# A two-layer hybrid decoder step on one Trainium2 core: zero rows beside the up projection's tiles, gap tiles back to back, and two of them moved into the up projection

## The chip, the core and the metric

The kernel runs on one core of a Trainium2 chip. Its engines are TensorE (PE), VectorE (DVE), ScalarE (ACT), GpSimd (POOL) and SyncE (SP), which here only issues loads; all DMAs, whoever issues them, run on the core's 16 DMA engines. The metric is the device time of one launch in microseconds. PE's granted clock is given as a share of 2.4 GHz; it has two levels, 1.0 (2.4 GHz) and 0.5 (1.2 GHz).

## The reference

One inference step of a two-layer decoder for a prompt of 256 tokens and 8 sample tokens, 264 columns together, width 1024, all in float32. Layer 0 mixes with gated linear attention and ends with a dense SwiGLU (the up projection has 2 x 2816 columns); layer 1 mixes with stick-breaking attention over shared keys and values (the samples' keys lie in a paged cache) and ends with eight SwiGLU experts, two for each token. Each norm is modulated by shift, scale and gate vectors, which are a matrix product of the conditioning vectors c.

```python
def modulate(h, shift, scale):
    return h * (1 + scale[:, None, :]) + shift[:, None, :]
def shared_kv(x, c, kv_norm, kv_ada_w, kv_ada_b, kv_w):
    shift, scale = jnp.split(jax.nn.silu(c) @ kv_ada_w + kv_ada_b, 2, axis=-1)
    h = modulate(rmsnorm(x, kv_norm), shift, scale)
    k, v = jnp.split(h @ kv_w, 2, axis=-1)
    ...
def swiglu(h, w_gate_up, w_down):
    a, b = jnp.split(h @ w_gate_up, 2, axis=-1)
    return (jax.nn.silu(a) * b) @ w_down
# trunk, for each layer
    sh1, sc1, g1, sh2, sc2, g2 = jnp.split(jax.nn.silu(c) @ p['ada_w'][layer] + p['ada_b'][layer], 6, axis=-1)
    h = modulate(rmsnorm(x, p['norm_mix'][layer]), sh1, sc1)
    ...
    x = x + g1[:, None, :] * out
    h = modulate(rmsnorm(x, p['norm_ffn'][layer]), sh2, sc2)
    ...
```

## The kernel before

Activations lie transposed, 8 chunks of 128 rows by 264 columns. **Weights** come through a ring of three buffers of 2 MB. The list `STREAM` gives the order of all tiles: `gla_in`, `gla_out`, `ffn_up` (11), `ffn_down` (6), `sb_q` (2), `kv` (4), `sb_out`, the cached keys and values, and 32 `ada` tiles of the conditioning product. SP walks through it in order; before each load it waits until the tile that had the buffer is used up (`read_out`), and every later load stands behind that wait.

A weight tile is cut into four **units**. ACT casts a unit to `w_hi` (L1247), DVE takes the rest `w_lo` (L1604), and PE multiplies it in three products (`three`, L733 to L735), 24 matmuls per unit. `AHEAD` is 3: units are split three ahead of their use. When the fourth unit of a tile has its `w_lo`, its ring buffer is free. Four PSUM banks (0 to 3) take turns as the products' targets.

An **ada tile** is read by PE as it is, in eight matmuls of 32 rows (L704, four for each half); ACT copies the sums to `ada_row` (L1263), which has two halves, PE turns them (four transpositions, L688), and DVE adds them up into `mod` (`ada_add`, L1620 and L1621) and counts up `ada_kept`. `ADA_GROUPS` gives the tiles their PSUM banks.

Ahead of the up projection, of `sb_q` and of `kv` (stages `FFN0`, `MIX1`, `KV`) there is a **gap**: squares and sums (L723) of the new x, then DVE (L1662, L1671) and ACT (L1302) make the normed input chunk by chunk. In the kernel before each gap holds two ada tiles (`BEHIND_SUMS`: 16, 18 and 20 are the first ones): PE reads the first and half of the second, waits for ACT's copy, turns it, reads the other half, and only then starts the projection; the second one is turned behind the projection's first block. `KV` has no sums of its own, and its gap stands behind the turning of the query (L935).

**POOL** sets eight parts of `routed` to zero (L568 to L571), 0.5 MB each, as soon as the up projection's input is done, one behind the other; then it makes constants for the attention. Later it stores the samples' query (L586), spreads its rows over the partitions (L595), and multiplies the second page of each sample's cached keys (L606), while DVE multiplies the first (L1883), sums both up (L1885, L1890) and splits the units of `kv` in between.

`ada_kept` must reach `ADA_NEEDED` for a stage: 20 for `KV`, 26 for `FFN1`.

## Time and profile before

| | |
|---|---|
| median of 3 runs | 1775.8 us (1775.76 to 1776.41) |
| the profiled execution's own time | 1775.7 us |
| its span, first to last instruction | 1774.0 us |
| PE busy | 1618.1 us, 91% |
| DVE, ACT, POOL busy | 71%, 61%, 5% |
| mean granted clock | 0.954 |
| DMA | 546.24 MB, 308 GB/s |

The stages in the trace: conditioning and linear attention to about 240 us, its output projection to 262, first gap, up projection from 276, down projection to 483, second gap, `sb_q` to 523, third gap and `kv` to 600, attention to 680, then router and experts to the end. A busy share is a mean over such stages; what a wait costs is read where it stands.

### The profile page before, as it was taken

The page shows a single profiled execution, that of the slowest core. Times are in us where ns is not written, and L with a number is a line of the kernel's source. Part 1 is how long each engine was busy: PE and PEld are TensorE (multiplying, and loading weights), DVE is VectorE, ACT ScalarE, POOL GpSimd, SP SyncE. Part 2 cuts the span into 40 slices and gives each one's busy share as a digit, 9 for nine tenths or more (in the row PEclk, how much of TensorE's full clock was granted, in tenths as well). Part 3 has the DMA queues.
Part 4 walks back from the last instruction along what each step waited for, and adds up shares of the span by engine and source line. Part 5 has one row for each costly group of instructions (what it writes and reads, how often), then busy time and mean ns, then how long its engine had stood idle before and what let it go on. Part 6 is the DMA issues. An engine that isn't in the chain of part 4 may idle for free.

```text
span 1774.0 us, 25158 instructions
## 1 busy us (share of the span) xinstructions
PE 1618.1 (91%) x9156; PEld 1308.3 (74%) x9156; DVE 1263.9 (71%) x1433; ACT 1079.6 (61%) x1309; POOL 88.9 (5%) x135
## 2 busy tenths in 40 slices
PE   5799786999986799599999999999999999999992
PEld 2695265999976667278888888888888888888882
DVE  2463354554565724389899899899998998998982
ACT  2553133443452453477777777777777777777771
POOL 2000101000002400100000000000000000000001
PEclk9899887999998899899999999999999999999995
DMA  9266977555557887699999999999999999999972
GB/s 347 76 211 231 387 262 257 188 174 177 178 190 289 321 323 255 251 352 361 369 378 375 376 369 377 380 371 366 382 372 372 373 376 380 367 366 387 373 279 97
DMA packets 241091, 546.24 MB, mean 308 GB/s; under 512 B 6131, under 2 KB 28785, under 8 KB 241026
## 3 DMA queue, kind: packets, MB, share of 16 engines
q1 hardware_dynamic: 229202, 504.42, 78.4%
q0 software_dynamic: 11184, 38.75, 5.9%
q10 hardware_dynamic: 640, 2.18, 0.4%
q8 instruction: 45, 0.74, 0.2%
q14 instruction: 20, 0.16, 0.0%
HBM read 522.56 MB, written 22.75 MB: 307 GB/s over the span
## 4 chain that ended last, share of the span: by engine, by line
PE 83%; DMA 7%; DVE 5%; ACT 3%; issue 2%; POOL 1%; SPq 0%; another core or an unknown queue 0%; ACTq 0%; DVEq 0%; POOLq 0%
PE psum L733 24%; PE psum L734 24%; PE psum L735 24%; DMA ring<-in_ada_w 3%; PE psum L704 2%; DMA ring<-in_cache_k 2%; PE psum L1168 1%; DMA ring<-in_ffn_w_gate_up 1%; PE psum L723 1%; DVE w_lo L1604 1%; DVE ring L1883 1%; DMA ring<-in_gla_w_in 1%; PE psum L688 1%; PE psum L972 1%; ACT w_hi L1247 0%
## 5 line engine op out<-in xcount | busy, mean ns | idle before, releaser
L2055 DVE TENSOR_TENSOR w_lo<-ring,w_hi 128x1024 fp32r<-128x1024 f32 x672 | 814.2, 1224 | 81.7 <-ACT w_hi L1546 64.7
L1546 ACT CAST w_hi<-ring 128x1024 fp32r<-128x1024 f32 x672 | 706.6, 1054 | 206.2 <-PE psum L735 200.1
L733 PE MATMUL psum<-w_hi,xe_hi 128*128 128x512 f32 x896 | 359.9, 402 | 3.2 <-DVE w_lo L2055 3.2
L735 PE MATMUL psum<-w_hi,xe_lo 128*128 128x512 f32 x896 | 355.8, 397 | 0.0
L734 PE MATMUL psum<-w_lo,xe_hi 128*128 128x512 f32 x896 | 355.7, 397 | 0.0
L733 PE MATMUL psum<-hh,w_hi 128*128 128x264 f32 x864 | 252.8, 293 | 32.4 <-DVE w_lo L1604 19.7
L1604 DVE TENSOR_TENSOR w_lo<-ring,w_hi 128x1024 fp32r<-128x1024 f32 (+1 forms) x132 | 160.2, 1222 | 151.6 <-ACT w_hi L1247 151.4
L734 PE MATMUL psum<-hl,w_hi 128*128 128x264 f32 x864 | 249.2, 288 | 0.0
L735 PE MATMUL psum<-hh,w_lo 128*128 128x264 f32 x864 | 249.1, 288 | 0.0
L1247 ACT CAST w_hi<-ring 128x1024 fp32r<-128x1024 f32 (+1 forms) x132 | 135.6, 1034 | 127.7 <-PE psum L735 86.0
L733 PEld LDWEIGHTS psum<-w_hi,xe_hi 128*128 128x128 f32 x896 | 169.3, 189 | 42.5 <-DVE w_lo L2055 3.5
L735 PEld LDWEIGHTS psum<-w_hi,xe_lo 128*128 128x128 f32 x896 | 169.1, 189 | 41.1
L734 PEld LDWEIGHTS psum<-w_lo,xe_hi 128*128 128x128 f32 x896 | 169.4, 189 | 38.8
L733 PEld LDWEIGHTS psum<-hh,w_hi 128*128 128x128 f32 x864 | 167.5, 194 | 39.6 <-DVE w_lo L1604 28.0
L733 PE MATMUL psum<-w_hi,at_hi 128*128 128x512 f32 x448 | 179.0, 399 | 0.0
L734 PE MATMUL psum<-w_lo,at_hi 128*128 128x512 f32 x448 | 177.5, 396 | 0.0
L735 PE MATMUL psum<-w_hi,at_lo 128*128 128x512 f32 x448 | 177.5, 396 | 0.0
L734 PEld LDWEIGHTS psum<-hl,w_hi 128*128 128x128 f32 x864 | 167.8, 194 | 0.0
L735 PEld LDWEIGHTS psum<-hh,w_lo 128*128 128x128 f32 x864 | 166.6, 193 | 0.0
L735 PEld LDWEIGHTS psum<-w_hi,at_lo 128*128 128x128 f32 x448 | 84.4, 188 | 20.6
L734 PEld LDWEIGHTS psum<-w_lo,at_hi 128*128 128x128 f32 x448 | 84.5, 189 | 19.8
L733 PEld LDWEIGHTS psum<-w_hi,at_hi 128*128 128x128 f32 x448 | 84.4, 188 | 19.8
(347 smaller groups left out, 1421.3 us busy)
## 6 DMA issues: line engine op xcount, KB each, us to landing
ring<-in_moe_w_gate_up SPq DMA_DIRECT2D x112, 2048.0 KB, 9.2
ring<-in_moe_w_down SPq DMA_DIRECT2D x56, 2048.0 KB, 8.4
ring<-in_ada_w SPq DMA_DIRECT2D x24, 2048.0 KB, 10.9
ring<-in_ffn_w_gate_up SPq DMA_DIRECT2D x22, 1024.0 KB, 8.9
ring<-in_gla_w_in SPq DMA_DIRECT2D x6, 2048.0 KB, 11.2
ring<-in_kv_ada_w SPq DMA_DIRECT2D x4, 2048.0 KB, 8.0
ring<-in_ffn_w_down SPq DMA_DIRECT2D x4, 2048.0 KB, 7.9
ring<-in_kv_w SPq DMA_DIRECT2D x4, 2048.0 KB, 12.8
```

What stands on the lines that cost most here:

```text
L688: last = eng.transpose(pb[ADA_BANKS[i]][:, j * P:(j + 1) * P], ada_row[:, i % 2, j * P:(j + 1) * P], ident[:])
L704: last = eng.matmul(pb[ADA_BANKS[i]][g * STRIP:(g + 1) * STRIP, :], c_pad[:, k, :], cols8(slot("ada", i))[:, k, :], start=j == 1, stop=j == 3)
L723: last = eng.matmul(pb[7][:, 0:T], ones[:], h[:, k, :], start=k == 0, stop=k == KC - 1)
L733: eng.matmul(to, wh, ah, start=start, stop=False)
L734: eng.matmul(to, wh, al, start=False, stop=False)
L735: return eng.matmul(to, wl, ah, start=False, stop=stop)
L972: eng.matmul(pb[2 * (g % 2) + a][:, 0:384], neg_after[:], lg[:, a, :], start=False, stop=False, skip_group_check=True)
L1168: last = eng.transpose(pb[4 if p % 2 == 0 else 7][:, j * CAP:(j + 1) * CAP], act_e[:, j * P:(j + 1) * P], ident[:])
L1247: eng.copy(unit(w_hi, kind, m, ks), quarter(slot(kind, i), kind, m % 4, ks)).then_inc(S["hi_ready"], 1)
L1546: eng.copy(unit(w_hi, kind, n), quarter(ring[(BASE + j // 4) % RING], kind, j % 4)).then_inc(S["hi_ready"], 1)
L1604: eng.tensor_tensor(unit(w_lo, kind, m, ks), quarter(slot(kind, i), kind, m % 4, ks), unit(w_hi, kind, m, ks), ALU.subtract).then_inc(S["l ...
L2055: eng.tensor_tensor(unit(w_lo, kind, n), quarter(ring[(BASE + j // 4) % RING], kind, j % 4), unit(w_hi, kind, n), ALU.subtract).then_inc(S ...
```

## The change

- `STREAM`: ada tiles 18 and 19 are loaded ahead of up tiles 4 and 7 (`BESIDE_UP`); 20 and 21 take their place between the two `sb_q` tiles; between the `kv` tiles there is none. So the ring buffers are dealt out anew.
- PE: in the gaps of `FFN0` and `MIX1` both ada tiles are read whole, one right behind the other, and turned behind the first and the second block of the projection (`turn_behind`). Tiles 18 and 19 are read at the head of up tiles 4 and 7 and turned behind the first block of these. The gap of `KV` has no ada tile.
- ACT and DVE: copies and sums follow, the first copy of a gap one chunk later.
- POOL: zero write e waits until the units ahead of up tile e + 2 are used.

```diff
--- before.py
+++ after.py
@@ -62,18 +62,19 @@
 ADA_ORDER = [*range(16), *range(24, 28), *range(16, 24), *range(28, 32)]
 
 
-ADA_GROUPS = ((0, (0, 1)), (4, (2, 3)), (16, (4, 5)), (18, (4, 5)), (20, (6, 7)), (22, (6, 7)), (28, (2, 3)))
-BEHIND_SUMS = {FFN0: 16, MIX1: 18, KV: 20}
+ADA_GROUPS = ((0, (0, 1)), (4, (2, 3)), (16, (4, 5)), (18, (4, 5)), (20, (4, 5)), (22, (6, 7)), (28, (2, 3)))
+BEHIND_SUMS = {FFN0: (16, 17), MIX1: (20, 21), KV: ()}
+BESIDE_UP = {4: 18, 7: 19}
 ADA_STARTS = [start for start, _ in ADA_GROUPS]
 ADA_BANKS = [[banks for start, banks in ADA_GROUPS if start <= i][-1][i % 2] for i in range(len(ADA_ORDER))]
 ADA_NEEDED = {MIX0: 4, FFN0: 12, MIX1: 16, KV: 20, FFN1: 26, FINAL: 32}
 
 STREAM = ([("ada", i) for i in range(4)] + [("gla_in", i) for i in range(6)] + [("ada", i) for i in range(4, 16)]
           + [("gla_out", i) for i in range(2)] + [("ffn_up", 0), ("ada", 16), ("ada", 17)]
-          + [("ffn_up", i) for i in range(1, 11)]
+          + [t for i in range(1, 11) for t in ([("ada", BESIDE_UP[i])] if i in BESIDE_UP else []) + [("ffn_up", i)]]
           + [("ffn_down", i) for i in range(6)]
-          + [("sb_q", 0), ("ada", 18), ("ada", 19), ("sb_q", 1)]
-          + [("kv", 0), ("ada", 20), ("ada", 21), ("kv", 1), ("k_cache", 0), ("kv", 2), ("k_cache", 1), ("kv", 3), ("k_cache", 2), ("k_cache", 3)]
+          + [("sb_q", 0), ("ada", 20), ("ada", 21), ("sb_q", 1)]
+          + [("kv", 0), ("kv", 1), ("k_cache", 0), ("kv", 2), ("k_cache", 1), ("kv", 3), ("k_cache", 2), ("k_cache", 3)]
           + [("ada", 22)] + [t for i in range(4) for t in (("ada", 23 + i), ("v_cache", i))] + [("ada", 27)]
           + [("sb_out", i) for i in range(2)] + [("ada", i) for i in range(28, 32)])
 TILE_AT = {k: n for n, k in enumerate(STREAM)}
@@ -568,6 +569,7 @@
             eng.memset(zero_rows[:], 0.0).then_inc(S["consts"], 1)
             eng.wait_ge(S["consts"], 12 + STRIPS)
             for e in range(NE):
+                eng.wait_ge(S["unit_used"], UNIT_AT["ffn_up", e + 2])
                 eng.dma_start(routed[e * T:e * T + CAP, :], zero_rows[0:CAP, :]).then_inc(S["routed_zero"], 16)
             eng.wait_ge(S["routed_zero"], 16 * NE)
             eng.tensor_copy(ident_r[:], ident[:]).then_inc(S["att_consts"], 1)
@@ -688,6 +690,30 @@
                     last = eng.transpose(pb[ADA_BANKS[i]][:, j * P:(j + 1) * P], ada_row[:, i % 2, j * P:(j + 1) * P], ident[:])
                 last.then_inc(S["ada_turned"], 1)
 
+            def ada_strips(i, half):
+
+                for g in range(STRIPS):
+                    k = half * STRIPS + g
+                    last = eng.matmul(pb[ADA_BANKS[i]][g * STRIP:(g + 1) * STRIP, :], c_pad[:, k, :],
+                                      cols8(slot("ada", i))[:, k, :], start=half == 0, stop=half == 1)
+                    if half == 1:
+                        last.then_inc(S["ada_done"], 1)
+
+            def ada_whole(i):
+                landed(eng, "ada", i)
+                ada_strips(i, 0)
+                ada_strips(i, 1)
+
+            def ada_behind(m):
+
+                eng.wait_ge(S["ada_kept"], BEHIND_SUMS[m][0])
+                for i in BEHIND_SUMS[m]:
+                    ada_whole(i)
+
+            def turn_behind(m, i):
+                if i < len(BEHIND_SUMS[m]):
+                    ada_turn(BEHIND_SUMS[m][i])
+
             def ada(lo, hi, ends=False):
 
                 for u in range(lo, hi):
@@ -699,12 +725,7 @@
                     if j == 1:
                         landed(eng, "ada", i)
                     if j % 2 == 1:
-                        for g in range(STRIPS):
-                            k = (j // 2) * STRIPS + g
-                            last = eng.matmul(pb[ADA_BANKS[i]][g * STRIP:(g + 1) * STRIP, :], c_pad[:, k, :],
-                                              cols8(slot("ada", i))[:, k, :], start=j == 1, stop=j == 3)
-                            if j == 3:
-                                last.then_inc(S["ada_done"], 1)
+                        ada_strips(i, j // 2)
                     if j == 1 and i not in ADA_STARTS:
                         ada_turn(i - 1)
                 if ends:
@@ -892,9 +913,18 @@
 
 
             sum_squares(FFN0)
-            ada(64, 72)
+            ada_behind(FFN0)
+
+            def behind_up(i):
+                turn_behind(FFN0, i)
+                if i % 4 == 0 and i // 4 in BESIDE_UP:
+                    ada_turn(BESIDE_UP[i // 4])
+
             for i in range(11):
-                project("ffn_up", i + 1, IN_FFN, first=i, then=lambda i: ada_turn(17) if i == 0 else None)
+                if i in BESIDE_UP:
+                    eng.wait_ge(S["ada_kept"], BESIDE_UP[i])
+                    ada_whole(BESIDE_UP[i])
+                project("ffn_up", i + 1, IN_FFN, first=i, then=behind_up)
             for i in range(2 * DOWN_ROWS):
                 half, r = i // DOWN_ROWS, i % DOWN_ROWS
                 ks = chunks_of("ffn_down", i)
@@ -914,8 +944,8 @@
 
 
             sum_squares(MIX1)
-            ada(72, 80)
-            project("sb_q", 2, IN_Q, then=lambda i: ada_turn(19) if i == 0 else None)
+            ada_behind(MIX1)
+            project("sb_q", 2, IN_Q, then=lambda i: turn_behind(MIX1, i))
 
             def turn_kv(i):
 
@@ -929,16 +959,12 @@
                 last.then_inc(S["kv_turned"], 1)
 
             eng.wait_ge(S["kept_act"], empt[BLOCK_AT["sb_q", 7]][1])
-            eng.wait_ge(S["ada_kept"], 20)
+            eng.wait_ge(S["ada_kept"], 22)
 
             for j in range(8):
                 last = eng.transpose(pb[4 + j // 4][0:NB, (j % 4) * P:(j % 4 + 1) * P], kvq[:, 16 + j, TP:T], ident[:])
             last.then_inc(S["qs_turned"], 1)
-            ada(80, 88)
-
             def behind_kv(i):
-                if i == 0:
-                    ada_turn(21)
                 if i in TURN_AFTER:
                     if TURN_AFTER[i] == 0:
                         eng.wait_ge(S["ada_kept"], 22)
@@ -1301,9 +1327,10 @@
                         eng.wait_ge(S["scaled"], m * KC + k + 1)
                         eng.activation(hh[:, k, 0:TP], h[:, k, 0:TP], ACT.Identity,
                                        bias=mod[:, SHIFT[m] + k, 0:1]).then_inc(S["hh_ready"], 1)
-                        if k == 3:
-                            ada_copy(BEHIND_SUMS[m])
-                    ada_copy(BEHIND_SUMS[m] + 1)
+                        if k == 4 and BEHIND_SUMS[m]:
+                            ada_copy(BEHIND_SUMS[m][0])
+                    for i in BEHIND_SUMS[m][1:]:
+                        ada_copy(i)
                     return
                 for k in range(KC + 1):
                     if k < KC:
@@ -1420,6 +1447,8 @@
             eng.wait_ge(S["state_stored"], 16)
             for i in range(FFC + 1):
                 if i < FFC:
+                    if i % 2 == 0 and i // 2 in BESIDE_UP:
+                        ada_copy(BESIDE_UP[i // 2])
                     got = block("ffn_up", 2 * i)
                     if i >= 2:
                         eng.wait_ge(S["kept_dve"], empt[BLOCK_AT["ffn_up", 2 * i - 4]][1])
@@ -1835,7 +1864,6 @@
                 add_block("gla_out", i, GATE[MIX0])
 
             norm(FFN0)
-            ada_add(16)
 
             for i in range(S0):
                 eng.wait_ge(S[f"s0_stored{i}"], 16 * len(range(i, NB, S0)))
@@ -1844,7 +1872,10 @@
                 if i < FFC:
                     n, u = BLOCK_AT["ffn_up", 2 * i + 1], UNIT_AT["ffn_up", i // 2] + i % 2 * 2
                     if i == 1:
+                        ada_add(16)
                         ada_add(17)
+                    if i % 2 == 1 and i // 2 in BESIDE_UP:
+                        ada_add(BESIDE_UP[i // 2])
                     split(u + AHEAD)
                     split(u + 1 + AHEAD)
                     eng.wait_ge(S["unit_used"], u + 2)
@@ -1861,17 +1892,16 @@
                 for j in range(4):
                     add_block("ffn_down", 4 * half + j, GATE[FFN0])
             norm(MIX1)
-            ada_add(18)
             link(eng.memset(zs, 0.0))
             eng.wait_ge(S["att_consts"], 4 + 2 * STRIPS)
             eng.tensor_copy(bias_r[:], sb_bias[:]).then_inc(S["bias_ready"], 1)
             eng.wait_ge(S["bias_ready"], 1)
             eng.tensor_tensor(bias_r[SD:P, :], sb_bias[SD:P, :], bias_r[SD:P, :], ALU.subtract).then_inc(S["bias_ready"], 1)
             split_during("sb_q", 1)
-            ada_add(19)
+            ada_add(20)
+            ada_add(21)
             split_during("sb_q", 2, first=1)
             norm(KV)
-            ada_add(20)
 
             by_head = lambda v: v.rearrange("p (h d) -> p h d", h=SH)
             page_of = lambda b, page: slot("k_cache", b // 2)[:, (b % 2 * 2 + page) * D:(b % 2 * 2 + page + 1) * D]
@@ -1890,8 +1920,6 @@
                 eng.tensor_reduce(zs[:, 1, b, 0:SH], by_head(page_of(b, 1)), AX.X, ALU.add).then_inc(S["z_s_ready"], 1)
 
             for u in range(16):
-                if u == 1:
-                    ada_add(21)
                 if u in PAGES_DURING:
                     page, b = PAGES_DURING[u]
                     (page1_scores if page else page0_scores)(b)
```

SP's order of loads from up tile 1 on (`in_kv_ada_w` is ada 18 and 19, `in_ada_w` x2 is 20 and 21), before:

```order
L460 DMA ring<-in_ffn_w_gate_up 128x8x256 x20
L464 DMA ring<-in_ffn_w_down 128x8x512 x2
...
L469 DMA ring<-in_sb_w_q 128x8x512
...
L455 DMA ring<-in_kv_ada_w 128x8x512
...
L469 DMA ring<-in_sb_w_q 128x8x512
L469 DMA ring<-in_kv_w 128x8x512
L455 DMA ring<-in_ada_w 128x8x512 x2
L469 DMA ring<-in_kv_w 128x8x512
L448 ISA
L448 DMA ring<-in_cache_k 128x1024
```

and of the changed kernel:

```order
L461 DMA ring<-in_ffn_w_gate_up 128x8x256 x6
...
L456 DMA ring<-in_kv_ada_w 128x8x512
L461 DMA ring<-in_ffn_w_gate_up 128x8x256 x6
...
L456 DMA ring<-in_kv_ada_w 128x8x512
L461 DMA ring<-in_ffn_w_gate_up 128x8x256 x8
...
L470 DMA ring<-in_sb_w_q 128x8x512
L456 DMA ring<-in_ada_w 128x8x512 x2
L470 DMA ring<-in_sb_w_q 128x8x512
L470 DMA ring<-in_kv_w 128x8x512 x2
L449 ISA
L449 DMA ring<-in_cache_k 128x1024
```

Two ada loads stand between up loads, and the first cached keys no longer stand behind a load that waits for the key projection.

PE between the first gap's sums and the first unit of the up projection, before:

```order
L723 MATMUL psum<-h,ones 128x264 x8
L704 MATMUL psum<-ring,c_pad 32x512 x12
L688 MATMUL psum<-ident,ada_row 128x128 x4
L704 MATMUL psum<-ring,c_pad 32x512 x4
L733 MATMUL psum<-hh,w_hi 128x264
```

and of the changed kernel:

```order
L744 MATMUL psum<-h,ones 128x264 x8
L697 MATMUL psum<-ring,c_pad 32x512 x16
L754 MATMUL psum<-hh,w_hi 128x264
L755 MATMUL psum<-hl,w_hi 128x264
L756 MATMUL psum<-hh,w_lo 128x264
```

The transposition is gone from between the ada matmuls, and the projection follows at once.

DVE from the last chunk of the key input to the first page product, before:

```order
L1671 SCALAR_TENSOR_TENSOR hl<-h,mod,hh 128x256 x2
L1620 TENSOR_REDUCE mod<-psum 128x36
L1621 TENSOR_TENSOR mod<-mod,vec_a 128x36
L1604 TENSOR_TENSOR w_lo<-ring,w_hi 128x1024
L1620 TENSOR_REDUCE mod<-psum 128x36
L1621 TENSOR_TENSOR mod<-mod,vec_a 128x36
L1883 TENSOR_TENSOR ring<-ring,h 128x1024
```

and of the changed kernel:

```order
L1700 SCALAR_TENSOR_TENSOR hl<-h,mod,hh 128x256 x2
L1633 TENSOR_TENSOR w_lo<-ring,w_hi 128x1024
L1913 TENSOR_TENSOR ring<-ring,h 128x1024
L1915 TENSOR_REDUCE work<-ring 128x16
L1633 TENSOR_TENSOR w_lo<-ring,w_hi 128x1024
```

Both sums are gone from there.

## Rows read from the trace of the kernel before

**Rows 1.** Windows: us, busy of each engine (instructions), PEclk, DMA share, GB/s.
```profile
289.40:299.60 10.20, 0.00 (x0) 0.03 (x1) 1.71 (x3) 2.78 (x4) 2.58 (x12) 0.61 1.07 355
299.60:483.20 183.60, 182.95 (x1488) 182.74 (x1488) 100.41 (x134) 79.94 (x110) 0.00 (x0) 0.98 0.59 194
...
522.70:555.70 33.00, 17.71 (x145) 14.04 (x144) 13.93 (x29) 12.44 (x23) 6.20 (x6) 0.83 0.68 252
```

**Rows 2.** Chain of waits, first gap and up projection: start us, us, what.
```profile
277.00 1.06 ACT w_hi L1247
...
278.17 1.24 DVE w_lo L1604
...
279.43 0.37 SPq L460
...
279.84 16.96 DMA ring<-in_ffn_w_gate_up
...
296.82 1.05 ACT w_hi L1247
...
299.61 0.56 PE psum L733
```

**Rows 3.** DMA queues, 278 to 298 us: packets, MB, share of 16 engines.
```profile
q0 software_dynamic: 1152, 4.19, 56.9%
q1 hardware_dynamic: 2799, 2.83, 41.7%
```

**Rows 4.** Up loads: 330 to 352 us (KB each, median us to landing), and line L460.
```profile
ring<-in_ffn_w_gate_up SPq DMA_DIRECT2D x4, 1024.0 KB, 6.8
...
DMA to landing us min/median/max: 5.2/8.9/19.2
```

**Rows 5.** Chain of waits, third gap and kv: start us, us, what.
```profile
533.59 0.37 SPq L469
...
535.88 15.26 DMA ring<-in_cache_k
551.16 1.24 DVE ring L1883
...
612.86 0.88 DVE work L1909
```

**Rows 6.** Second gap and sb_q: timelines of SP and DVE, line L469 at 500, chain.
```profile
500.38 0.37 SPq L469 DMA_DIRECT2D ring<-in_sb_w_q  x1
...
501.42 3.58 SPq L455 DMA_DIRECT2D ring<-in_ada_w  x1
...
DMA to landing us min/median/max: 8.1/8.1/8.1
...
497.11 0.48 DVE L1671 SCALAR_TENSOR_TENSOR hl<-h,mod,hh 128x256 fp32r<-128x256 f32 x1 [0.18 <-ACT hh L1302]
...
510.83 0.39 PE psum L733
```

**Rows 7.** Timeline of PE: a half ada tile, a turn, and the end of sb_q.
```profile
626.64 1.06 PE L704 MATMUL psum<-ring,c_pad 128*32 128x512 f32 x8
...
627.64 0.43 PE L956 MATMUL psum<-bias_r,sixty_fourth 128*128 128x384 f32 x1
...
501.48 0.60 PE L688 MATMUL psum<-ident,ada_row 128*128 128x128 f32 x4
501.83 0.37 PE L733 MATMUL psum<-hh,w_hi 128*128 128x264 f32 x1
...
522.61 0.14 PE psum L735
```

**Rows 8.** Windows of 2 us around the hole at 290, columns as in rows 1.
```profile
290.00:292.00 2.00, 0.00 (x0) 0.00 (x0) 0.00 (x0) 0.00 (x0) 0.00 (x0) 0.91 1.07 370
...
304.00:306.00 2.00, 2.00 (x13) 2.00 (x13) 0.00 (x0) 0.74 (x2) 0.00 (x0) 0.68 1.10 348
```

**Rows 9.** GpSimd's query rows: timeline, landing (530 to 550 us), landing in the whole kernel.
```profile
534.10 1.12 POOL L595 DMA_DIRECT2D h<-q_scratch  x2 [1.86 <-DMA q_scratch<-work]
...
DMA to landing us min/median/max: 7.7/9.2/10.7
...
DMA to landing us min/median/max: 3.6/5.5/10.7
```

## The prediction

> **What bounds the kernel now.** I read the page's 40 slices first: PE is busy nearly everywhere, with dips around 280 to 300 us and 520 to 600 us. The expert loop behind 760 us runs whole and isn't touched, so only the stretch from 262 to 614 us counts, and everything later moves with it.
>
> The windows by stage give the sizes [rows 1]. From 289.40 to 299.60 PE does no matmul at all, while the DMA engines run at a share of 1.07. From 299.60 to 483.20 PE is busy for 182.95 of 183.60 us: up and down projection are bound by PE. From 522.70 to 555.70 PE works 17.71 of 33.00 us.
>
> The chain of waits names the cause of the first hole [rows 2]. ACT and DVE split the last quarter of up tile 0, which frees its ring slot. SP issues up tile 1 at 279.43, its load takes 16.96 us from 279.84, and PE resumes only at 299.61. In the same stretch GpSimd's queue writes the zero rows, 4.19 MB in eight DMAs, against 2.83 MB of loads [rows 3]. Later, with nothing beside them, up loads land in a median of 6.8 us [rows 4].
>
> The chain also names the second hole [rows 5]. SP issues key tile 1 at 533.59, and behind it the first cached key pages, whose load is the 15.26 us to 551.16, where DVE begins the page products. From there to the first softplus at 612.86 the chain is almost all DVE products, reductions and splits, with a page load between.
>
> **The change, part by part.** Times of before are of the profiled execution, 1775.7 us (span 1774.0), against a median of 1775.8; the two agree, so differences go straight onto the median.
>
> (1) Zero rows. Each of the eight writes now waits until an up tile is used (tiles 1 to 8), so none lies beside up tile 1. Behind these waits GpSimd has only the remaining writes and the constants of the attention; they are wanted at about 498 us, and the last wait ends near 400. The load of up tile 1 is issued at about 279.0: ACT's copy of the second ada tile no longer waits for PE, which brings its next split forward by 0.4 us, and DVE's behind it [rows 2]. The load then takes between 6.8 us (the later median) and 13.6 us (twice that, since two more tiles are queued behind it on the same queue). sb_q tile 1 shows the nearest case, three 2 MB tiles the first issued at 500.38 and the last at 501.42, the first landing 8.1 us after its issue [rows 6]. I take 8. It lands at 287.0, and from the landing to PE's first matmul there were 2.79 us (296.82 to 299.61) [rows 2]. PE resumes at 289.8 instead of 299.61: 9.8 us. I keep 9.5, because both ada additions now stand on DVE in front of the next split (0.5 us, half of it behind PE).
>
> (2) Both gap tiles back to back in the first gap. PE's first up unit was held until 276.3 by the transposition and the last four ada matmuls; now it starts with the first ready chunk, near 271.5, and ends with the last chunk, near 277. With 3.0 us per unit (seven units in the 20.9 us from 501.83 to 522.70 [rows 7]) and two transpositions of 0.35 us, PE has used units 0 to 3 by 286.8. The tile lands later than that, so this part is worth nothing in time. It is hidden under the load.
>
> (3) Ada tiles 18 and 19 inside the up projection. PE is the bound there, so this is a full price. Four ada matmuls (eight records, two for each in fp32) hold PE for 1.0 us (626.64 to 627.64) and a transposition for 0.35 (501.48 to 501.83) [rows 7]: per tile 2 x 1.0 + 0.35, for two tiles 4.7 us. The new waits: PE's for the sums of the tile before is met a tile earlier; ACT's copy waits for the last ada matmul, and behind it stands a split that PE wants three units on, 2.0 + 0.6 + 1.05 + 1.23 = 4.9 us against 2.0 + 9.0. ACT's copy and DVE's sum fit into their idle time, each of them being busy for about half of this stretch (79.94 and 100.41 of 183.60 us [rows 1]). Where they were, behind the sums of the key input, PE had nothing else to do, so taking them out there returns nothing on PE.
>
> The loads: with an ada tile in a ring of three, an up tile is often issued when the tile two before it has been split, not three. From the split of a tile's last unit to that of the first unit two tiles later lie five units, 14.5 us, plus 6.4 us of units split ahead (three units less a split's 2.3 us). Loads of this kind took 5.2 to 19.2 us, the longest beside the zero rows [rows 4]; a 0.5 MB write beside each adds some 1.5 us. Nothing waits: cost 0, the cover being the 20.9 us.
>
> (4) Gap of sb_q. Tiles 20 and 21 are now read back to back, their turns lie behind units 0 and 1, and PE's wait ahead of the query's turning is for sums that DVE has by 514 us, nine before it gets there. PE's first unit is paced by DVE's last chunk at 497.11 to 497.59 [rows 6] and ends near 498.0; units 1 to 3 and both turns end at 507.7. But unit 4 needs sb_q tile 1, issued at 500.38 after a split; the split comes 0.45 us sooner, so unit 4 starts at 510.3 instead of 510.8. Earlier PE just met it; now it idles 2.6 to 3 us. Idle time has a price in the clock. After 289.4 the granted clock fell to the lower level (1.2 GHz) within 290 to 292, and after the restart at 299.61 it came back only within 304 to 306 [rows 8]. Such a low stretch, some 5.7 us, costs 2.8 us at half speed. Here it would come on the path. Between -0.45 (no fall) and +2.4 (a full one) I take +1.0. The Trainium skill, "TensorE: Matmul & The Clock Gate", Part 1, speaks against this edit in the same way: the gate goes to half rate after idling, and where it falls is run-variable because the monitor runs free. By that page either end can come, -0.45 or +2.4; the trace agrees that idling brings the lower level, and no run yet shows how the fall varies.
>
> (5) Key gap. The key tiles 0 and 1 and the first key pages no longer stand behind ada tiles 20 and 21. Key pages 0 take the slot of sb_q tile 1, free at about 515, behind 6 MB that runs out near 518, so they land near 524 instead of 551.16. What is late next is the queries' rows: the products need them spread over all partitions, and GpSimd stores the query only after ACT's two copies. One ada copy ahead of these is gone (0.46 us), so the row loads start at 533.65 instead of 534.10. Before, the three loads of that place landed 7.7, 9.2 and 10.7 us after issue, the first being the one that is needed; over the whole kernel such loads range from 3.6 to 10.7 with a median of 5.5 [rows 9]. I take 7.5, a little under the row of this place: DVE starts at 541.1 instead of 551.16, 10.0 us earlier. With 5.5 it is 12, with 10.7 it is 6.8. Everything up to 612.86 is the same sequence on DVE, with the same loads issued from the same releases, and moves whole.
>
> A rule of the skill sharpens this price: "DMA: Bandwidth & Descriptors", Queues, rings and completion order, says an engine round-robins between queues packet by packet. A row load then shares with one load on SP's queue as badly as with three queued there, so the landing stays 7.7 us and the gain 9.8, not 12. The trace agrees so far as two queues were served side by side in the first hole, 4.19 MB and 2.83 MB over the same 20 us [rows 3].
>
> Sum: -9.5 + 4.7 + 1.0 - 10.0 = -13.8 us. 1775.8 - 13.8 = 1762.
>
> **The rivals.**
> A: the query rows become late. At a landing of 10.7 us the fifth part gives 6.8, and 1765; if they needed 17.5 us nothing would be left of it, and 1772. For it: three loads on a second queue landed 7.7 to 10.7 us after issue. Against: there were 6 MB beside them, now 2. Chance 0.08 for a time of 1766 to 1772.
>
> B: the zero writes do their harm again, 0.5 MB at a time. Eight writes at about 350 GB/s are 1.5 us each, 12 us if all lay on the path: 1774, no change. For: the same engines. Against: the loads of the up projection are idle for part of each tile (194 GB/s used [rows 1], up to 350 to be had), so only with the prefetch gone would it show. Chance 0.04.
>
> C: slower than before, one mechanism: the ring. Ada tiles 18 and 19 take a buffer each, six up tiles have only 20.9 us of cover. It decides from a landing above that: at 23.2 us the six waits eat the 13.8 us, at 25 they cost 6 x 4.1 = 24.6 us and give 1786. For: 19.2 us occurred. Against: that was beside all zero rows at once; the median is 8.9 [rows 4]. Chance 0.05.
>
> D: the clock does better. If the hole behind unit 3 of the up projection is short enough for no fall (3 us by my count, 286.8 to 289.8), another 2.8 us go, and without a fall in sb_q 1.4 more: 1758. If in addition the query rows land in 5.5 us, 1756. Chance 0.2.
>
> **How the numbers follow.** Forecast as it stands (1759 to 1766) 0.63, A 0.08, B 0.04, C 0.05, D 0.2. The predicted time is 1762. The range 1755 to 1769 holds the forecast, D and half of A, some 0.87 by these counts, less what I haven't thought of. A change under 0.2% (3.6 us) couldn't be told from none. Faster by more: forecast, D, and most of A, 0.91. Within: 0.04. Slower: 0.05.
>
> **What would show it.** The load of up tile 1 at about 8 us with no write beside it, and PE's hole behind unit 3 at 3 us instead of 10.2; if the load still takes over 13 us, the zero rows were not the cause. Sixteen ada matmuls and eight transposition matmuls between up tiles, the up and down projection longer by 4.7 us, without a new idle of PE for a split; a wait of ACT for up loads there means C. A short idle of PE between the fourth and fifth unit of sb_q, with the granted clock behind it. DVE's first page product released by the query rows and not by the key pages, at about 10 us less behind the last chunk of the key input, and the same 61.7 us from there to the first softplus. Wrong would be a key page load that still releases it, or a gain of under 6 us there.

## The result, and the profile after

The changed kernel takes 1760.03 us (median of 4 runs, 1758.68 to 1763.92) against 1776.1 us for the kernel before in the same series (4 runs, 1775.76 to 1776.41): a ratio of 0.9914, interval 0.9902 to 0.9926. The forecast was 1762. The profiled execution took 1761.09 us, its span being 1759.3 us, 14.7 us less than the span before.

The chain of waits in the first gap of the changed kernel (start us, us, what) answers to [rows 2]:

```profile
276.45 0.95 ACT w_hi L1273
...
277.53 1.24 DVE w_lo L1633
278.78 0.37 SPq L461
...
279.19 7.78 DMA ring<-in_ffn_w_gate_up
287.00 1.05 ACT w_hi L1273
...
289.79 0.36 PE psum L754
```

The load of up tile 1 takes 7.78 us, not 16.96. The DMA queues from 278 to 298 us (packets, MB, share of 16 engines) say why: GpSimd's queue q0, 4.19 MB there in [rows 3], is gone, and SP's queue moves 6.20 MB in place of 2.83.

```profile
q1 hardware_dynamic: 6137, 6.20, 96.7%
q8 instruction: 1, 0.02, 0.4%
```

The windows over PE's hole, over up and down projection, and over the key gap, with the columns of [rows 1]:

```profile
286.80:289.80 3.00, 0.02 (x2) 0.04 (x1) 1.73 (x3) 2.80 (x4) 0.00 (x0) 1.00 1.10 348
289.80:475.90 186.10, 185.45 (x1528) 182.07 (x1528) 101.47 (x141) 80.91 (x112) 7.54 (x20) 1.00 0.70 237
516.20:540.20 24.00, 14.78 (x105) 12.69 (x105) 13.13 (x25) 11.73 (x21) 6.21 (x6) 0.94 0.44 156
```

The hole is 3.0 us and the granted clock in it stays at 1.00; before it was 10.2 us at 0.61. The 186.1 us behind it hold 40 more matmul records (1528 against 1488): four fp32 ada halves and two turns. PE stays busy for 185.45 of them.

One of the two ada tiles, in PE's timeline (start us, us, engine, line, operation); its neighbours are up matmuls on both sides, with no idle time in front:

```profile
324.54 0.28 PE L756 MATMUL psum<-hh,w_lo 128*128 128x264 f32 x1
324.76 1.92 PE L697 MATMUL psum<-ring,c_pad 128*32 128x512 f32 x16
...
326.61 0.39 PE L754 MATMUL psum<-hh,w_hi 128*128 128x264 f32 x1
326.84 0.28 PE L755 MATMUL psum<-hl,w_hi 128*128 128x264 f32 x1
...
329.52 0.28 PE L756 MATMUL psum<-hh,w_lo 128*128 128x264 f32 x1
329.64 0.60 PE L690 MATMUL psum<-ident,ada_row 128*128 128x128 f32 x4
330.00 0.37 PE L754 MATMUL psum<-hh,w_hi 128*128 128x264 f32 x1
330.21 0.28 PE L755 MATMUL psum<-hl,w_hi 128*128 128x264 f32 x1
```

In sb_q PE now idles before unit 4, where before it just met it (510.83 in [rows 6]). PE's timeline, and windows of 2 us behind it:

```profile
502.70 0.39 PE L754 MATMUL psum<-hh,w_hi 128*128 128x264 f32 x1 [2.08 <-DVE w_lo L1633]
```

```profile
502.00:504.00 2.00, 1.30 (x7) 1.30 (x8) 2.00 (x3) 2.00 (x4) 0.00 (x0) 0.77 1.06 388
504.00:506.00 2.00, 2.00 (x11) 2.00 (x10) 1.93 (x6) 1.07 (x2) 0.00 (x0) 0.50 1.05 385
506.00:508.00 2.00, 2.00 (x17) 2.00 (x16) 1.13 (x1) 0.56 (x2) 0.00 (x0) 0.88 1.05 386
```

The idle time is followed by a stretch at the lower clock level, 1.2 GHz. Against the full clock these windows lose 2 x (0.23 + 0.50 + 0.12) = 1.7 us.

In the key gap the chain no longer goes through the key pages ([rows 5]) but through the query's store and row loads (start us, us, what):

```profile
524.55 2.67 DMA q_scratch<-work
...
527.51 8.03 DMA h<-q_scratch
...
535.62 1.24 DVE ring L1913
...
551.16 6.78 DMA ring<-in_cache_k
...
573.60 6.60 DMA ring<-in_cache_k
...
597.89 0.88 DVE work L1937
```

The stretch as a whole, cut at marks that are the same instructions in every kernel: "sums 1" is PE's first squares matmul behind gla_out, "resume" its first matmul of up tile 1, "sums 2" the first one behind the down projection, "key input" DVE's first operation on it (h<-x,rstd), "page" the first page product, "softplus" the first softplus. Times are differences between row starts of the timelines, in us of one profiled execution each; of after they are 262.12, 289.79, 475.92, 516.21, 535.62 and 597.81.

| kernel | sums 1 to resume | to sums 2 | to key input | to page | to softplus | sum |
|---|---|---|---|---|---|---|
| before | 37.44 | 183.62 | 39.60 | 28.33 | 61.62 | 350.61 |
| after | 27.67 | 186.13 | 40.29 | 19.41 | 62.19 | 335.69 |
| difference | -9.77 | +2.51 | +0.69 | -8.92 | +0.57 | -14.92 |

The whole difference of the spans is in this stretch. It is also a better ruler than the total, which went from 1773.16 to 1778.61 us over the 30 runs of the kernel before in the experiments' series. But each sum is one execution, and a fall of the clock inside it moves it by some 1.5 to 2.6 us (e10).

### The profile page after: what moved, and what is told of

It is laid out like the page before. It is cut to its first block, busy times and chain, and to the rows that moved or that the text cites. A ratio compares the mean times of both kernels' runs of the same rounds, so it can differ in the third digit from the quotient of the medians.

```text
span 1759.3 us, 25141 instructions
## 1 busy us (share of the span) xinstructions
PE 1618.5 (92%) x9156; PEld 1307.5 (74%) x9156; DVE 1262.0 (72%) x1433; ACT 1078.2 (61%) x1309; POOL 89.4 (5%) x135
## 4 chain that ended last, share of the span: by engine, by line
PE 76%; issue 9%; DMA 7%; DVE 4%; ACT 2%; POOL 1%; SPq 0%; POOLq 0%; ACTq 0%; DVEq 0%
PE psum L754 22%; PE psum L755 22%; PE psum L756 22%; DMA ring<-in_ada_w 3%; PE psum L697 2%; PE psum L1194 1%; DMA ring<-in_gla_w_in 1%; DVE ring L1913 1%; DVE w_lo L1633 1%; DMA ring<-in_cache_k 1%; PE psum L744 1%; PE psum L998 1%; PE psum L690 1%; DMA routed<-h_tok,row_of 1%; PE psum L1188 1%
```

## The experiments

Totals are medians; each ratio is to the kernel before in the same series, whose median was 1774.89 us for e1 to e4, 1775.31 for e5 to e8 and 1776.06 for e9 to e11; "sum" is the stretch from sums 1 to softplus as above.

| run | total (lowest to highest) | ratio to before, interval | sum |
|---|---|---|---|
| e1 zero wait alone | 1762.97 (1761.97 to 1765.33) | 0.9934 [0.992, 0.9947] | 339.55 |
| e2 zero rows at once | 1770.77 (1769.27 to 1772.35) | 0.9975 [0.9964, 0.9985] | 346.58 |
| e3 turn in the gap | 1759.81 (1758.64 to 1760.28) | 0.9911 [0.9896, 0.9926] | 334.30 |
| e4 tiles back | 1763.66 (1762.67 to 1768.41) | 0.9942 [0.9928, 0.9955] | 338.67 |
| e5 zero rows twice | 1758.98 (1757.35 to 1763.34) | 0.9916 [0.9902, 0.9929] | 335.62 |
| e6 kept busy | 1763.07 (1761.74 to 1763.61) | 0.9928 [0.9914, 0.9941] | 335.23 |
| e7 query early | 1752.82 (1750.12 to 1754.07) | 0.9872 [0.9857, 0.9887] | 329.23 |
| e8 split early | 1752.82 (1751.34 to 1753.82) | 0.9872 [0.9857, 0.9887] | 329.01 |
| e9 both | 1746.58 (1745.79 to 1748.17) | 0.9836 [0.9823, 0.985] | 319.31 |
| e10 rows behind the tile | 1760.12 (1759.74 to 1762.1) | 0.991 [0.9897, 0.9924] | 335.02 |
| e11 both, turn in the gap | 1750.5 (1746.45 to 1752.84) | 0.9848 [0.9833, 0.9862] | 326.20 |

**e1: the zero wait alone**, on the kernel before.

```diff
             for e in range(NE):
+                eng.wait_ge(S["unit_used"], UNIT_AT["ffn_up", e + 2])
                 eng.dma_start(routed[e * T:e * T + CAP, :], zero_rows[0:CAP, :]).then_inc(S["routed_zero"], 16)
```

> The kernel before with one edit: each zero write waits until up tile e + 2 is used. Theory (the zero rows held up tile 1): the load falls from 16.96 us to about 8, the tile is there at 287.9, and PE, which ends unit 3 at 289.4, resumes near 290.6 instead of 299.61: 9 us; with a hole of 1.2 us instead of 10.2 the clock has no reason to fall, another 2.8 us. Together 9 to 12 us: 1764 to 1767. Rival (the load is slow because two more 2 MB tiles are queued behind it, 13 us or more): the tile lands at 293 or later, and the gain is under 4 us: 1772 or more.

The load took 7.88 us. PE's timeline has a hole of 1.18 us, and the windows over the hole and over up and down projection read, with the columns of [rows 1]:

```profile
290.15 0.36 PE L734 MATMUL psum<-hh,w_hi 128*128 128x264 f32 x1 [1.18 <-DVE act L1855]
```

```profile
288.90:290.10 1.20, 0.08 (x1) 0.00 (x0) 1.20 (x3) 1.20 (x3) 0.00 (x0) 1.00 1.10 347
290.10:471.20 181.10, 180.39 (x1488) 180.20 (x1488) 100.44 (x135) 80.00 (x110) 8.79 (x20) 1.00 0.65 220
```

The same 1488 matmuls that took 182.95 us at a clock of 0.98 take 180.39 at 1.00. So one line is worth 11.1 us of the sum: 9.1 of load (37.44 to 28.35) and 2.5 of clock (183.62 to 181.07), less 0.6 elsewhere. The total, 1762.97 us, lies 1 us under the expected 1764 because the kernel before took 1774.89 us in this series; the gain, 11.9 us, is within the expected 9 to 12. The rival fell.

**e2: the zero rows at once**, the added wait of e1 taken out of the changed kernel.

```diff
-                eng.wait_ge(S["unit_used"], UNIT_AT["ffn_up", e + 2])
```

> The changed kernel without the waits of the zero writes, so all eight are issued right behind the last chunk of the up projection's input. Theory: the load of up tile 1 takes 16 to 17 us again instead of 7.8, PE resumes at 296 + 2.8 = 299 instead of 289.8, 9 us, and the clock falls in a hole of 12 us, 2.8 us more: 1769 to 1772. Rival (the new order of the gap shortened the load, not the writes): the load stays near 8 us and the time near 1760.

4.19 MB of zeros lie beside 2.30 MB of loads again, and PE idles for 12.67 us. PE's timeline, and windows of 2 us in the hole:

```profile
301.15 0.56 PE L753 MATMUL psum<-hh,w_hi 128*128 128x264 f32 x1 [12.67 <-DVE act L1884]
```

```profile
290.00:292.00 2.00, 0.00 (x0) 0.00 (x0) 0.00 (x0) 0.00 (x0) 0.00 (x0) 0.66 1.04 413
292.00:294.00 2.00, 0.00 (x0) 0.00 (x0) 0.00 (x0) 0.00 (x0) 0.00 (x0) 0.50 1.03 332
```

The sum is 10.9 us longer than after's, 9.67 to the resume and 1.4 behind it. The new order of the gap did nothing for the duration of the load.

**e3: the turn in the gap**, the changed kernel with the old order inside the first two gaps.

```diff
-            ada_behind(FFN0)
+            ada(64, 72)
...
-            ada_behind(MIX1)
+            ada(80, 88)
```

(and the turns, copies and sums of these tiles where they were)

> The changed kernel with the old order inside the first two gaps: the first ada tile is turned between the halves of the second, and only the second one's turn lies behind unit 0. Theory: worth nothing in the first gap, since up tile 1 lands at 287 either way (PE ends unit 3 near 289 instead of 286.8, and the hole of 3 us closes); in the gap of sb_q PE ends unit 3 some 2 us later, just in time for tile 1, and with no hole the clock stays up. So 1760 less 0 to 1.5 us, and a smaller spread than the 5 us of the changed kernel. Rival (back to back tiles start the units earlier and this is kept): 2 to 3 us slower, 1762 to 1763.

PE's hole in the up projection shrinks to 0.74 us and the one in sb_q is gone; there the clock stays at 1.00 from 496 to 508. The total is the same as after's within its spread, 1759.81 against 1760.03, and the rival (2 to 3 us slower) fell. The sum is 1.4 us shorter. PE resumes 0.65 us later behind sums 1, because up tile 1 is issued 17.26 us behind them and not 16.66; the key input is reached 0.7 us sooner behind sums 2, and the page product 1.0 sooner behind that, half of it the row's landing (7.51 us). So back to back tiles brought 0.6 us in the first gap and cost 0.7 in the second: as long as the next tile was late, they mostly turned paced work into idle time.

**e4: the tiles back**, ada tiles 18 and 19 in the gap of sb_q, 20 and 21 in the key gap.

```diff
-BEHIND_SUMS = {FFN0: (16, 17), MIX1: (20, 21), KV: ()}
-BESIDE_UP = {4: 18, 7: 19}
+BEHIND_SUMS = {FFN0: (16, 17), MIX1: (18, 19), KV: (20, 21)}
+BESIDE_UP = {}
```

> The changed kernel with ada tiles 18 and 19 in the gap of sb_q and 20 and 21 in the key gap again (back to back, turned behind the next units); nothing lies in the up projection. Theory: up and down projection 5.3 us shorter, and the first page product again released by the key pages' load, 8.9 us later: 1760 + 3.6 = 1763.6. Rival A (what the two tiles cost on PE in the up projection is more than their matmuls, through the ring): the up projection gets shorter by more than 5.3 us, and the whole is no slower than 1760. Rival B (the gain of the key gap came from elsewhere): the page product is not late, and the time is near 1755.

1763.66, as the theory had it. From the resume to sums 2 it takes 181.05 us (e1: 181.07), so the two tiles cost 186.13 - 181.06 = 5.1 us in the up projection, and nothing through the ring. The key pages' load is back in the chain, and the page product is 28.3 us behind the key input, not 19.4:

```profile
523.98 15.11 DMA ring<-in_cache_k
```

In sb_q PE idles here for 2.28 us, a little longer than in after, and yet the granted clock stays at 1.00 behind it (PE's timeline and a window):

```profile
498.82 0.39 PE L754 MATMUL psum<-hh,w_hi 128*128 128x264 f32 x1 [2.28 <-DVE w_lo L1635]
```

```profile
500.00:502.00 2.00, 2.00 (x19) 2.00 (x18) 1.93 (x5) 1.20 (x2) 0.00 (x0) 1.00 1.05 386
```

From sums 2 to the key input it takes 38.96 us, 1.3 us less than after.

**e5: the zero rows twice**, a second 0.5 MB behind each write.

```diff
+                eng.dma_start(expert_out[e * CAP:(e + 1) * CAP, :], zero_rows[0:CAP, :]).then_inc(S["routed_zero"], 16)
```

> The changed kernel with each zero write doubled (a second 0.5 MB behind it, of the same zeros, into rows that are rewritten later). Theory (the loads of the up projection have cover enough): nothing waits, 1760 within 1 us. Rival B (a write beside an up load delays PE): what eight more writes of 1.5 us cost, up to 12 us, 1772.

The sum is 335.62 against 335.69. Rival B of the prediction fell.

**e6: kept busy**, extra matmuls in PE's two holes.

```diff
+            def keep_busy(n):
+                for _ in range(n):
+                    eng.matmul(pb[6][:, 0:P], ones[:], ident[:], start=True, stop=True)
```

> The changed kernel with extra matmuls, whose sums nobody reads, in PE's two holes: 12 of 128 columns in fp32 behind unit 3 of the up projection (some 2.5 us of the 3) and 8 behind unit 3 of sb_q (1.7 us of 2.1). Theory (an idle of 2 us brings the lower clock in some executions): the granted clock stays at 1.00 from 500 to 508 us, where it cost 0.23 + 0.50 + 0.12 of 2 us each = 1.7 us, so 1758.3, and the runs lie within 2 us of each other instead of 5. Rival (the clock falls for what lies earlier, in the paced first unit of sb_q, not for the hole): 1760 and the same spread.

Half right, and the half that is right isn't shown to come from the matmuls. The windows in sb_q show the full clock with 16 records of extra matmuls ahead of them, where after had 0.77 and 0.50:

```profile
502.00:504.00 2.00, 0.46 (x5) 0.27 (x3) 1.25 (x2) 2.00 (x4) 0.00 (x0) 1.00 1.06 389
504.00:506.00 2.00, 1.97 (x16) 1.97 (x17) 2.00 (x2) 2.00 (x4) 0.00 (x0) 1.00 1.04 384
```

But in e4 and e10 the clock stayed up behind unfilled holes of 2.28 and 1.91 us, so one execution doesn't show that the extra matmuls held it; they end ahead of the landing, and 1.57 us of the hole are left. And in this execution sb_q tile 1 landed later (ACT had waited 10.12 us for it, 8.84 in after), and only 0.5 us of the sum is left of the gain. The total is not better but 3 us worse, and the stretch to softplus doesn't hold those 3 us; they lie later, around the router (the chain reaches the first expert matmul at 742.97, after's at 739.37), where its chain of waits has a piece "another core or an unknown queue" of 4.55 us. Why isn't settled. The five runs lie within 1.9 us of each other, as the theory had it; but e10, with its holes, stays within 2.4 us and e11, without them, spreads over 6.4, so the scatter isn't shown to come from the holes. From softplus to the end of the span alone the profiled runs differ by 4.5 us (1159.35 in e1, 1163.89 here).

**e7: the query early**, ACT's two copies of the query inside the loop over the key input's chunks.

```diff
+                        if m == KV and k == 1:
+                            eng.wait_ge(S["qs_turned"], 1)
+                            eng.copy(qs_tok[:, 0:512], pb[4][0:NB, :])
+                        if m == KV and k == 3:
+                            eng.copy(qs_tok[:, 512:D], pb[5][0:NB, :]).then_inc(S["qs_kept"], 1)
```

> The changed kernel with ACT's two query copies inside the loop over the key input's chunks (behind chunks 1 and 3) instead of behind chunk 7, so that the query is stored while the chunks are still made. Theory (the query rows release the first page product): the store is done before the last chunk, the row loads are issued at 523.9 instead of 527.5 and the page product starts at 532 instead of 535.6, 3.6 us; ACT's copies hold some chunks back by up to 0.6 us. 1756.5 to 1757. Rival A (a key page or a split is late next): under 1 us gained. Rival B (the delayed chunks reach PE and the splits behind): no gain or slower.

Twice the expected gain: the page product is 12.38 us behind the key input, not 19.41. 3.1 us are the earlier issue (8.18 us behind the key input, 11.30 in after), 3.9 a landing of 4.1 instead of 8.0, which the expectation did not have. What the row loads wait for is now DVE's last chunk and no longer the store. In after SP's key tile 2 was issued at 526.49, a microsecond ahead of the rows at 527.51. Here the order is the other way round (timelines of GpSimd, SP and DVE, one kernel):

```profile
523.68 1.12 POOL L597 DMA_DIRECT2D h<-q_scratch  x2 [2.89 <-DVE hl L1702]
...
524.82 0.39 SPq L470 DMA_DIRECT2D ring<-in_kv_w  x1
...
527.88 1.23 DVE L1915 TENSOR_TENSOR ring<-ring,h 128x1024 f32<-128x1024 f32 x1 [3.08 <-DMA h<-q_scratch]
```

**e10: the rows behind the tile**, e7 with the row loads held until the split that releases key tile 2.

```diff
+            eng.wait_ge(S["lo_ready"], UNIT_AT["kv", 0] + 4)
             for b in range(Q_ROWS - 1):
                 load_q(b)
```

> The kernel with the early query copies, but GpSimd's row loads wait for the split that releases key tile 2, so they are issued beside or just behind that 2 MB load (524.8) instead of 1.1 us ahead of it (523.7). Theory (what the loads wait for is the 2 MB tile issued first: the row took 8.0 us behind it in the changed kernel and 4.1 us ahead of it in this one): the landing goes back to about 8 us, the page product starts at 532.5 instead of 527.9, 4 to 5 us for a delay of 1.1: 1757. Rival (the landing was short for another reason, such as the store being long done): 4 us again, 1 us slower than with the early copies alone, 1754.

```profile
527.75 0.39 SPq L470 DMA_DIRECT2D ring<-in_kv_w  x1
...
528.31 1.12 POOL L597 DMA_DIRECT2D h<-q_scratch  x2 [4.59 <-DVE w_lo L1636]
...
536.05 1.23 DVE L1916 TENSOR_TENSOR ring<-ring,h 128x1024 f32<-128x1024 f32 x1 [8.33 <-DMA h<-q_scratch]
```

The store had been issued 5.2 us earlier (it took 2.67 us in after), and still the row took 7.65 us (chain of waits), 0.56 us behind the tile. From the key input to the page product it is 17.62 us against 12.38: 1.7 us of later issue and 3.5 of landing. The rival fell: what is issued first decides. The other profiled executions agree. With the rows 1.1 us ahead of the tile they landed in 4.10, 4.14 and 4.17 us (e7, e9, e11), with the rows 0.5 to 1.0 us behind it in 7.51 to 8.19 us (after, e3, e5, e6, e8, e10).

The total, 1760.12 us, is 3 us above the expected 1757. One piece of it lies elsewhere: from the resume to sums 2 this execution takes 188.79 us, where every other one with the same matmuls and a short hole or none takes 186.05 to 186.15. PE's hole in the first gap is as long as after's, but here the clock fell behind it, and in sb_q, where it fell in after, it did not (38.84 us from sums 2 to the key input). PE's timeline, and windows behind the hole:

```profile
290.80 0.56 PE L755 MATMUL psum<-hh,w_hi 128*128 128x264 f32 x1 [2.88 <-DVE act L1888]
```

```profile
290.00:292.00 2.00, 1.21 (x5) 1.24 (x6) 1.93 (x7) 2.00 (x4) 0.00 (x0) 0.50 1.10 347
294.00:296.00 2.00, 2.00 (x11) 2.00 (x11) 1.63 (x3) 0.00 (x0) 0.00 (x0) 0.50 1.09 346
```

Against e7 the two together make 1.1 us of the sum; the rest of the 3 us isn't located. After's sum and this one's are alike (335.69 and 335.02) only because such pieces cancel.

**e8: the split early**, unit 3 of up tile 0 and of sb_q tile 0 split between ACT's squares.

```diff
+                    if k == 6:
+                        for n in EARLY.get(m, ()):
+                            split(n, late=True)
                     eng.activation(h[:, k, :], x[:, k, :], ACT.Square).then_inc(S["squared"], 1)
```

(and on DVE ahead of its wait for the sums)

> The changed kernel with the split of unit 3 of up tile 0 and of sb_q tile 0 made in the gap before, between ACT's squares 5 and 6 and, on DVE, ahead of the mean, both idle there. Up tile 1 is then issued near 266 instead of 278.8, sb_q tile 1 near 480 instead of 492.6. Theory: both holes of PE go, 3.0 and 2.1 us, and with the second one the low clock behind it (1.7 us): 1760 - 5 to -6.8, 1753 to 1755. Rival (two more 2 MB tiles beside the first make it land no earlier than PE needs it, or the split delays the sums): a gain under 2 us.

SP issues up tile 1 3.8 us behind sums 1 (261.52), in after it was 16.7, and PE is busy for 199.83 of the 201.40 us from its first up matmul to sums 2. SP's timeline (one row for six DMAs) and the window:

```profile
265.32 12.80 SPq L463 DMA_DIRECT2D ring<-in_ffn_w_gate_up  x6
```

```profile
270.70:472.10 201.40, 199.83 (x1632) 194.99 (x1632) 108.61 (x155) 89.45 (x125) 8.49 (x21) 1.00 0.68 229
```

The sum is 6.7 us shorter: 3.2 up to sums 2, 2.6 in the gap of sb_q, 1.0 behind the page product. The rival fell; neither the sums nor the first landing suffered.

**e9: both**, the edits of e7 and e8 together.

> The changed kernel with both edits together: the splits of unit 3 made in the gaps before, and the query copies inside the chunk loop. Theory (separate places on the path): from the sums of the first gap to the first softplus 335.7 us less 6.5 (query) and less 6.7 (splits), 322.5 us, and 1746 to 1747 in all. Rival (with the early splits sb_q ends sooner and the key pages come to be late instead of the query rows): 2 us or more of it are lost, 1749.

1746.58 us, the best version, 13.5 us below the changed kernel. The sum is 319.31, 3.2 us below what the two gains add up to, since the key input is reached 1.2 us sooner behind sums 2 than in e8 (there the clock is at 0.50 to 0.67 from 482 to 490 us; here it is back at 1.00 from 488 on) and the two page loads behind the first product land faster (6.13 and 6.10 us against 6.78 and 6.60 in after; chain of waits):

```profile
518.08 4.14 DMA h<-q_scratch
522.30 1.24 DVE ring L1922
...
537.93 6.13 DMA ring<-in_cache_k
...
559.70 6.10 DMA ring<-in_cache_k
...
582.16 0.88 DVE work L1946
```

**e11: both, with the turn in the gap**, the edit of e3 on top of e9.

> Both edits as before, and the first two gaps in the old order: the first ada tile turned between the halves of the second. Theory (back to back tiles were worth nothing only because up tile 1 was late): now no tile is late, PE starts the units at 276.5 instead of 271 and ends unit 3 at 290.0 instead of 286.8, 3 us in each of the two gaps: 5 to 6 us slower than with both edits alone, near 1752. Rival (the order of the gap never matters): the same time as with both edits.

Slower than e9 by 3.9 us in the median and 6.9 in the sum, of which 2.5 lie up to sums 2 and 1.9 in the gap of sb_q; the rest, 2.4, is behind the page product. The profiled execution is the slowest of the five, and two of the five (1746.45 and 1746.83) are as fast as e9's, so it is the 2.5 and 1.9 us at their marks that show it, 4.4 of the expected 5 to 6: with no tile late, the order of the gap counts. Each of the two is from one pair of executions.

## Why the prediction was right

| step | forecast | measured | by |
|---|---|---|---|
| 1 and 2: load of up tile 1, order of the first gap | -9.5 | -9.8 | after; e1, e2, e3 |
| 3: two ada tiles in the up projection | +4.7 | +5.1 | e1, e4 |
| the clock behind the first hole (rival D) | 0 | -2.5 | e1 |
| 4: gap of sb_q | +1.0 | +0.7 | after; e4, e10 |
| 5: key gap | -10.0 | -8.9 | after; e4 |
| page product to softplus | 0 | +0.6 | after |
| sum | -13.8 | -14.9 | |

The mechanism of every step came as forecast. That the sum is within 1.1 us is in part luck: 2.5 us of clock that it did not count, and 0.3 us each in steps 1 and 4, stand against 2.1 us by which the up projection, the key gap and the stretch behind it came out worse.

**Step 1** held in its mechanism and its number: the load at 7.78 us against 8. e1 and e2 make and unmake it with one line. 9.2 of the 9.8 us are the load, 0.6 its earlier issue (16.66 us behind sums 1 against 17.26), for which the forecast had 0.4.

**Step 2** was called worth nothing because it is hidden under the load. e3 shows that up to the 0.6 us of the earlier issue, and e11 shows the other half: uncovered, the same edit is worth some 2.5 and 1.9 us in the two gaps.

**Step 3** was 0.4 us too small for two tiles. The tile's sixteen records take 1.85 us to the next up matmul (324.76 to 326.61) and the turn 0.36, 2.2 per tile, a little less than the 2.35 of the forecast, 4.4 for both. The rest is at the joints. Up matmuls start 0.12 us apart; the last one ahead of the tile is 0.22 us ahead of it, and the first one behind it holds PE for 0.23, that behind the turn for 0.21 (330.00 to 330.21). From 324.54 to 326.84 and from 329.52 to 330.21, less four starts of 0.12, are 2.5 us per tile, 5.0 for both. It isn't idle time: PE is idle for 0.65 us of the stretch, for 0.71 in e1. The ring held, so rival C fell.

**Rival D** had the clock stay up, and the runs show that this is not settled by the program: after, e7 and e10 are the same up to the key input, and yet their clocks differ. The two holes, with the lowest clock in the windows of 2 us behind them and the time of the stretch that pays for it:

| execution | hole, first gap | clock | resume to sums 2 | hole, sb_q | clock | sums 2 to key input |
|---|---|---|---|---|---|---|
| after | 2.98 | 1.00 | 186.13 | 2.08 | 0.50 | 40.29 |
| e5 | 2.87 | 1.00 | 186.15 | 2.36 | 0.50 | 40.55 |
| e7 | 2.92 | 1.00 | 186.15 | 2.23 | 0.57 | 40.43 |
| e4 | 2.88 | 1.00 | 181.05 (no ada tiles) | 2.28 | 1.00 | 38.96 |
| e10 | 2.88 | 0.50 | 188.79 | 1.91 | 1.00 | 38.84 |
| e2 | 12.67 | 0.50 | 187.56 | 2.15 | 0.50 | 40.39 |

Behind a hole of 2.9 us in the first gap the clock fell in one execution of five, behind one of 1.9 to 2.4 us in sb_q in four of six. The first half of the rival, priced at 2.8 us, came true beside the forecast in after's profiled execution, with 2.5; this is the largest single miss of the sum, and it had been priced, just not taken. In e10 it would not have come. The second half did not come in after, but did in e4 and e10.

**Step 4**: the idle came (2.08 us, forecast 2.6 to 3), and in after the lower clock behind it. The forecast weighed no fall (-0.45) against a full one (+2.4) and took +1.0 between them. The two cases lie nearer together: against the 39.60 us of before, the executions without a fall are at -0.6 and -0.8, those with one at +0.7 to +1.0. So a fall costs some 1.5 us here and not 2.85, and +1.0 was close because it is what a fall gives. e3, which has neither the idle nor a fall behind it, takes 39.57 us, as much as before.

**Step 5** named the right next wait. It was 1.1 us too large: the store was issued 0.48 us sooner, as said, but landed 0.5 us later than before (2.96 us from its issue to that of the rows, 2.45 before), and the row took 8.03 us where 7.5 was taken. The landing stayed near the 7.7 us of this place in [rows 9] though 6 MB beside it had become 2. The prediction had worked that out from the rule of the Trainium skill, "DMA: Bandwidth & Descriptors", Queues, rings and completion order, that an engine takes turns between queues, packet by packet; the trace agrees so far, with 8.03 us. But the count of rivals isn't all: e7 and e10 show 4.1 us for rows issued 1.1 us ahead of the 2 MB tile and 7.65 us for rows 0.56 us behind it. Which of the two goes first was half of what could be had here.

Rivals A and B didn't come: the rows landed well under 10.7 us, and doubled zero writes cost nothing.

The total moved by 16.1 us and the stretch by 14.9. The rest is within the scatter of the total and isn't explained by a step.

## What to carry to other kernels

When a load is late, ask first what shares the DMA engines with it, and then which instruction's end lets it be issued: here one moved wait took 9 us off the load, and a split done a gap earlier took the remaining hole away. An edit that is hidden under a late load is worth next to nothing until the load is fixed, so try it again behind every fix. Of two transfers released within a microsecond of each other, make sure that the one on the path is issued first. And look at the clock behind every hole before comparing two executions: the same hole of 2 to 3 us cost nothing in one and 1.5 to 2.6 us in another.

## What the runs showed of the hardware

- PE's idle of 10.2 and 12.7 us in the first gap was followed by the lower clock level (0.50 in the windows), idle of 0.74 and 1.2 us there was not. In between it varied from execution to execution: behind 2.9 us the clock fell once in five (e10), behind 1.9 to 2.4 us in sb_q four times in six. The length of the idle time alone doesn't tell, and no run shows what does. Nor is it shown that useless matmuls in the hole prevent the fall: the clock stayed at 1.00 with them (e6), but also without them (e4, e10).
- A fall cost 2.6 us in the first gap (e10 against after) and some 1.5 us in sb_q (e4 and e10 against after, e2, e5 and e7).
- 0.5 MB on GpSimd's queue landed in 4.1 to 4.2 us when issued 1.1 us ahead of a 2 MB load on SP's queue (three executions), and in 7.5 to 8.2 us when issued 0.5 to 1.0 us behind one (six).
- Between up matmuls that start 0.12 us apart, sixteen ada records and a turn of four cost 2.5 us, 0.3 of it at the joints.
- Doubling eight 0.5 MB writes spread over the up projection changed the stretch by less than 0.1 us.
